# Who rounds and modulates the expert tokens: a second half moved to VectorE, a modulation spread over four steps

## What is computed

```python
def moe_swiglu(h, router_w, router_b, wg, wu, wd):
    logits = (h @ router_w).astype(jnp.float32) + router_b.astype(jnp.float32)
    top_val, top_idx = lax.top_k(logits, TOP_K)
    top_w = jax.nn.softmax(top_val, axis=-1)
    ...
    out = jnp.zeros_like(h)
    for e in range(N_EXPERTS):
        out = out + gates[..., e:e + 1] * swiglu(h, wg[e], wu[e], wd[e])
    return out
```

## Time and profile before

| | us |
|---|---|
| time, median of 3 runs (2276.32 to 2282.88) | 2277.53 |
| the profiled execution: its time | 2279.8 |
| the profiled execution: its span | 2278.0 |
| TensorE busy | 2151.4 (94% of the span) |
| VectorE busy | 1745.4 (77%) |
| ScalarE busy | 1329.2 (58%) |
| GpSimd busy | 116.7 (5%) |
| weight remainders on VectorE, L3227, 288 of 2.29 us | 654.8 |
| weight roundings on ScalarE, L2231, 288 of 1.91 us | 549.6 |

### The profile page before, as it was taken

One profiled execution on the slowest core, in us unless ns is written; L12 is line 12 of the kernel. 1 busy time (PEld: TensorE's weight loads), 2 busy tenths in 40 slices (PEclk: granted clock), 3 DMA queues, 4 the chain that ended last, 5 costly groups with the idle time before them and its releaser, 6 DMA issues.

```text
span 2278.0 us, 30568 instructions
## 1 busy us (share of the span) xinstructions
PE 2151.4 (94%) x11791; PEld 1825.7 (80%) x11791; DVE 1745.4 (77%) x1729; ACT 1329.2 (58%) x1394; POOL 116.7 (5%) x141
## 2 busy tenths in 40 slices
PE   6999989899999999999988799999999999999995
PEld 5977878789888696998876688888888888888884
DVE  6467677667774664677868688888998989898896
ACT  4654435555434423443563577777777777777774
POOL 2000000000010010001000100000000000000000
PEclk8999989999999999999999799999999999999998
DMA  8754663447876312768645599999999999999994
GB/s 324 261 188 166 214 220 138 153 156 254 300 264 244 128 63 75 268 234 303 226 172 202 207 369 357 397 348 403 350 396 356 392 362 381 374 375 375 370 379 165
DMA packets 249440, 621.27 MB, mean 273 GB/s; under 512 B 13658, under 2 KB 22213, under 8 KB 249285
## 3 DMA queue, kind: packets, MB, share of 16 engines
q1 hardware_dynamic: 229444, 530.28, 63.6%
q0 software_dynamic: 16864, 81.86, 10.2%
q10 hardware_dynamic: 3042, 7.88, 0.9%
HBM read 611.60 MB, written 12.58 MB: 274 GB/s over the span
## 4 chain that ended last, share of the span: by engine, by line
PE 79%; DVE 11%; ACT 4%; DMA 3%; issue 2%; POOL 0%; DVEq 0%; POOLq 0%; ACTq 0%
PE ps L1531 24%; PE ps L718 15%; PE ps L1536 12%; PE ps L760 8%; PE ps L741 5%; DVE ada L2273 2%; ACT w_high L2231 2%; DVE ring_low L2264 2%; PE ps L803 2%; DMA slab<-in_w_ada 1%; DVE arena L2264 1%; PE ps L1502 1%; DVE arena L3188 1%; DVE arena L2273 1%; DMA arena<-in_w_ada 1%
## 5 line engine op out<-in xcount | busy, mean ns | idle before, releaser
L3227 DVE TENSOR_TENSOR w_low<-ring,w_high 128x2048 fp32r<-128x2048 f32 x288 | 654.8, 2287 | 92.0 <-PE ps L1536 71.9
L2231 ACT CAST w_high<-ring 128x2048 fp32r<-128x2048 f32 x288 | 549.6, 1914 | 198.0 <-PE ps L1536 182.0
L1580 ACT CAST part_high<-ring 128x1024 fp32r<-128x1024 f32 x287 | 297.0, 1049 | 328.0 <-PE ps L760 137.7
L2264 DVE TENSOR_TENSOR ring_low<-ring,part_high 128x1024 fp32r<-128x1024 f32 x287 | 340.0, 1217 | 153.8 <-ACT part_high L1580 152.2
L1531 PE MATMUL ps<-w_high,tokens_hl 128*128 128x512 f32 x1792 | 449.3, 393 | 5.7 <-POOL tokens_hl L647 5.7
L1531 PEld LDWEIGHTS ps<-w_high,tokens_hl 128*128 128x128 f32 x1792 | 334.3, 188 | 74.6 <-issue 5.5
L760 PE MATMUL ps<-part_high,arena_split 128*128 128x512 f32 x752 | 237.7, 398 | 14.1 <-DVE arena_split L2264 6.1
L1536 PE MATMUL ps<-w_low,tokens_hl 128*128 128x512 f32 x896 | 240.2, 390 | 0.9 <-DVE w_low L3227 0.9
L1531 PE MATMUL ps<-w_high,hidden_hl 128*128 128x512 f32 x896 | 224.4, 392 | 0.0
L1536 PEld LDWEIGHTS ps<-w_low,tokens_hl 128*128 128x128 f32 x896 | 168.1, 188 | 37.1 <-DVE w_low L3227 1.4
L1531 PEld LDWEIGHTS ps<-w_high,hidden_hl 128*128 128x128 f32 x896 | 166.4, 188 | 34.4
(11 more groups left out here) (293 smaller groups left out, 2447.1 us busy)
## 6 DMA issues: line engine op xcount, KB each, us to landing
ring<-in_moe_w_gate SPq DMA_DIRECT2D x96, 1024.0 KB, 7.0
ring<-in_moe_w_up SPq DMA_DIRECT2D x96, 1024.0 KB, 6.8
ring<-in_moe_w_down SPq DMA_DIRECT2D x96, 1024.0 KB, 7.1
slab<-in_ada_w POOLq DMA_DIRECT2D x64, 768.0 KB, 5.6
ring<-in_w_in SPq DMA_DIRECT2D x22, 2048.0 KB, 8.9
ring<-in_w_ff SPq DMA_DIRECT2D x16, 2048.0 KB, 8.7
hT<-in_moe_w_up SPq DMA_DIRECT2D x16, 1024.0 KB, 6.9
hT<-in_moe_w_gate SPq DMA_DIRECT2D x16, 1024.0 KB, 7.3
```

The source lines that it names most:

```text
L1580: L(nc.scalar.copy(o, i), s)
L2231: nc.scalar.copy(high, whole).then_inc(sem("high_ready"), 1)
L2264: L(V.tensor_tensor(o, a, b, op), s)
L3227: V.tensor_tensor(low, whole, high.bitcast(F32), ALU.subtract).then_inc(sem("low_ready"), 1)
```

## The change

Four things are moved.

- **The first tokens' second half.** GpSimd rounds only tiles 0 to 3 of the first round's tokens. VectorE rounds tiles 4 to 7 and forms their remainder, behind its own modulation and ahead of its first weight remainder.
- **The modulation of the next round's tokens.** At steps 33 to 36 ScalarE modulates tiles 0 to 3, one per step, and VectorE tiles 4 to 7, one per step. ScalarE waits for the turned tokens (`gathered`) at step 33. At step 37 it also waits for its own last weight rounding (`high_ready`), by which its tiles are written.
- **The token remainders.** The first half stands at m = 38 as before, the second at m = 39.
- **Routing.** The first three count products signal `routed` 2 by themselves; the other two go to another PSUM bank and signal 3. The reduction of the counts on VectorE follows the selection instead of standing ahead of it, and waits for 3. An equality test and a product, one behind the other, become one operation for each of the two token tiles.

```diff
-            for h in range(2):
-                four = slice(4 * h, 4 * h + 4)
-                pool.wait_ge(sem("gathered_ready"), h + 1)
-                nc.gpsimd.tensor_copy(tokens_hl[:, 0, four], A(EG, KT, P)[:, four]).then_inc(sem("tokens_high"), 1)
-                pool.wait_ge(sem("tokens_high"), h + 1)
...
+            four = slice(0, 4)
+            pool.wait_ge(sem("gathered_ready"), 1)
+            nc.gpsimd.tensor_copy(tokens_hl[:, 0, four], A(EG, KT, P)[:, four]).then_inc(sem("tokens_high"), 1)
+            pool.wait_ge(sem("tokens_high"), 1)
...
-            pe.matmul(ps[:, 1, 8:16], con("until"), mask[:, 1, :], start=False, stop=True)
-            pe.matmul(ps[:, 1, 16:24], ones, mask[:, 0, :], start=True, stop=False)
-            pe.matmul(ps[:, 1, 16:24], ones, mask[:, 1, :], start=False, stop=True).then_inc(sem("routed"), 1)
+            pe.matmul(ps[:, 1, 8:16], con("until"), mask[:, 1, :], start=False, stop=True).then_inc(sem("routed"), 1)
+            pe.matmul(ps[:, 7, 0:8], ones, mask[:, 0, :], start=True, stop=False)
+            pe.matmul(ps[:, 7, 0:8], ones, mask[:, 1, :], start=False, stop=True).then_inc(sem("routed"), 1)
...
+            def modulated(n, k):
+
+                act.wait_ge(sem("gathered"), n)
+                nc.scalar.activation(A(EG, KT, P)[:, k, :], ps[:, 0, k * P:(k + 1) * P], ACT.Identity,
+                                     scale=shift[:, 1, k:k + 1], bias=shift[:, 1, KT + k:KT + k + 1])
...
+                    if 33 <= m < 37:
+                        modulated(i + 3, m - 33)
                     if m == 37:
+                        act.wait_ge(sem("high_ready"), i * E_STEPS + (m + 1))
                         gathered_high(i + 3)
...
-                tt(eq, lg, top[i].unsqueeze(2).broadcast_to([P, 2, 8]), ALU.is_equal)
-                L.settle()
-                tt(eq, eq, rank, ALU.mult)
+                for t in range(TT):
+                    stt(eq[:, t, :], lg[:, t, :], top[i][:, t:t + 1], con("eight_down"), ALU.is_equal, ALU.mult)
...
-            L(V.tensor_reduce(best[:, 0:1], ps[:, 1, 16:24], AX.X, ALU.max))
...
             build_selection(0).then_inc(sem("selected"), 1)
+            dve.wait_ge(sem("routed"), 3)
+            L(V.tensor_reduce(best[:, 0:1], ps[:, 7, 0:8], AX.X, ALU.max))
...
-                modulate(h + 1, range(4 * h, 4 * h + 4))
+                modulate(h + 1, range(4 * h, 4 * h + 4)).then_inc(sem("gathered_ready"), 1)
+            dve.wait_ge(sem("gathered_ready"), 2)
+            dve.wait_ge(sem("tokens_low"), 1)
+            V.tensor_copy(tokens_hl[:, 0, 4:8], gathered[:, 4:8]).then_inc(sem("tokens_high"), 1)
+            dve.wait_ge(sem("tokens_high"), 2)
+            V.tensor_tensor(tokens_hl[:, 1, 4:8], gathered[:, 4:8], tokens_hl[:, 0, 4:8].bitcast(F32), ALU.subtract
+                            ).then_inc(sem("tokens_low"), 1)
...
-                    if m == 36:
-                        modulate(i + 3, range(KT))
-                    if m == 38:
-                        gathered_low(i + 3)
+                    if 33 <= m < 37:
+                        ins = modulate(i + 3, (m - 29,))
+                        if m == 36:
+                            ins.then_inc(sem("gathered_ready"), 1)
+                    if m in (38, 39):
+                        gathered_low(i + 3, slice(4 * (m - 38), 4 * (m - 37)))
```

More of the change, by code:

```diff
@@ L640, in _ @@
                                                 ).then_inc(sem("kv_scaled"), 1)
-            for h in range(2):
-                four = slice(4 * h, 4 * h + 4)
-                pool.wait_ge(sem("gathered_ready"), h + 1)
-                nc.gpsimd.tensor_copy(tokens_hl[:, 0, four], A(EG, KT, P)[:, four]).then_inc(sem("tokens_high"), 1)
-                pool.wait_ge(sem("tokens_high"), h + 1)
-                nc.gpsimd.tensor_tensor(tokens_hl[:, 1, four], A(EG, KT, P)[:, four], tokens_hl[:, 0, four].bitcast(F32),
-                                        ALU.subtract).then_inc(sem("tokens_low"), 1)
+            four = slice(0, 4)
+            pool.wait_ge(sem("gathered_ready"), 1)
+            nc.gpsimd.tensor_copy(tokens_hl[:, 0, four], A(EG, KT, P)[:, four]).then_inc(sem("tokens_high"), 1)
+            pool.wait_ge(sem("tokens_high"), 1)
+            nc.gpsimd.tensor_tensor(tokens_hl[:, 1, four], A(EG, KT, P)[:, four], tokens_hl[:, 0, four].bitcast(F32),
+                                    ALU.subtract).then_inc(sem("tokens_low"), 1)
             pool.wait_ge(sem("vector2"), 6)
@@ L3189, in modulate, with gathered_low @@
                                           shift[:, 1, k:k + 1], shift[:, 1, KT + k:KT + k + 1], ALU.mult, ALU.add)
-                ins.then_inc(sem("gathered_ready"), 1)
-            def gathered_low(n):
+                return ins
+            def gathered_low(n, four):
                 dve.wait_ge(sem("tokens_high"), n)
-                for four in (slice(0, 4), slice(4, 8)):
-                    V.tensor_tensor(tokens_hl[:, 1, four], A(EG, KT, P)[:, four], tokens_hl[:, 0, four].bitcast(F32),
-                                    ALU.subtract).then_inc(sem("tokens_low"), 1)
+                V.tensor_tensor(tokens_hl[:, 1, four], A(EG, KT, P)[:, four], tokens_hl[:, 0, four].bitcast(F32),
+                                ALU.subtract).then_inc(sem("tokens_low"), 1)
             def copy_output(n_done, moved):
@@ L3232, in _ @@
                     if m == 12:
[L3233 removed]
+                        dve.wait_ge(sem("routed"), i + 4)
                         V.tensor_copy(rounds[:, 2 + 2 * TT:3 + 2 * TT], ps[:, 4, 0:1]).then_inc(sem("slot_tokens"), 1)
```

2 lines of the change are left out of this document (1 added, 1 removed).

## The result

| | us |
|---|---|
| changed kernel, median of 6 runs (2252.53 to 2264.65) | 2261.07 |
| kernel before beside it, median of 6 runs (2270.67 to 2282.88) | 2276.82 |
| ratio, with its 95% interval | 0.9941 [0.9921, 0.9962] |
| the profiled execution of the changed kernel: time, span | 2252.53, 2250.7 |

The kernel is faster, by 13.4 us as the ratio has it (8.7 to 18.0). 17.2 us had been forecast, as 2260.3 us.

The account below looks back on a forecast made before the run. TensorE was taken as the bound, with only small gaps to win: 6.0 us at the first round's start plus 11.2 in the rounds, 17.2 off 2277.5, gives 2260.3 us; range 2255 to 2268.

Parts of the forecast that it names:

- 11.2 forecast: Steps 37 to 39 of all eight rounds: the three stalls go, minus 11.2 us.
- the new wait of ScalarE: Step 33: ScalarE's first tile waits for the tokens turned by TensorE, 1.6 us once per round.
- the cover: Step 34: VectorE's remainder waits for TensorE until about 1385.7 anyway, so ScalarE's delay of 1.3 us stays hidden.
- No stall moved elsewhere: Rival, steps 38 to 40: token remainders cost 0.5 us per round, 4 us stay in, 2264.3 us; chance 0.12.
- DMA did not take over: Rival, rounds: DMA limits at 374 GB/s, a round stays at 120.4 us, only 6.0 won, 2271.5; chance 0.06.
- ScalarE did not become the bound: Rival, steps 33 to 37: table loads with the tiles make ScalarE the bound, 10.8 us slower, 2288.3; chance 0.03.
- The term of 6.0 us: First round's start: step 6 starts at about 1301.5 instead of 1307.47, minus 6.0 us.
- The start's own chain: First round: weight remainders start at 1283.72 against 1283.67, step 1 at 1287.15 instead of 1292.30.
- the full clock: First round's step 1, behind a gap of about 2 us: full clock taken, step 2 at 1289.87 instead of 1296.59.
- a sign of being wrong: Half clock in the first round's step 1; step 6 then at 1302.3, the start giving minus 5.2 us.
- The pairs of small routing operations: Routing: two dependent pairs become independent ones, 0.25 us instead of 0.38 each, so 0.26 go.
- the lower bound of 0.49: VectorE's new 128x512 rounding at the start: bounds 0.49 and 0.68 us, 0.49 taken.

Follow-up runs that it names:

- the run with extra tiles: Changed kernel, but ScalarE computes each of its four tiles three more times into places nobody reads; rounds of 120.27 us, 1.23 us lost per round.
- The experiment with the start alone: Changed kernel with the loop put back: changed routing and first tokens' rounding, rounds as before; 2269.82 us beside 2275.13, ratio 0.9968.
- the run with the rounding alone: Kernel before with only the rounding of the first tokens' second half moved to VectorE, routing and rounds as before; one run of 2270.97 us.
- the run with the order enforced: Kernel before plus one wait: VectorE waits, ahead of its first weight remainder, for GpSimd's second rounding; one run of 2271.17 us.

## Why the prediction was right, and where it was not

**The rounds: right in mechanism and size.** 11.35 us were won of 11.2 forecast, nearly all in steps 37 to 40. Of the working, step by step: the new wait of ScalarE 1.68 us (forecast 1.6), a tile on ScalarE 0.46, as in the earlier trace rows; VectorE's remainder of step 34 still waits for TensorE and not for ScalarE, so the cover held; the smallest spare time 1.1 us (step 40 of the first round) for a forecast 1.3. The remainder of step 37 started at 1378.42, for about 1378.7 forecast on this trace's scale (step 37 starts 15.63 us earlier here). No stall moved elsewhere. What the prediction did not see is that parts of this were not needed: once the modulation is spread, a round stays at 119.04 to 119.06 us without the second engine, and without the split of the token remainders (both left out at once was not tried).

**DMA did not take over.** The rounds moved 378 and 383 GB/s where the earlier trace rows has 374, and no wait of a weight rounding ended on a DMA. The 358 GB/s of the Trainium skill's page "DMA: Bandwidth & Descriptors" (Specifications), read as the prediction does as a limit of this core, would have held the round at 120.4 us or more; the trace disagrees by 20 to 25 GB/s.

**ScalarE did not become the bound,** by nearly 3 us of room per round, as the run with extra tiles showed. No table load came with the tiles.

**The start: right in this pair of traces, mis-sized for the kernel.** The term of 6.0 us took the start in the earlier trace rows as what the kernel before always does. It was one of two courses, and in the two further profiles of it the 7.01 us rounding was 0.60, and step 6 stood 5.5 us earlier. From those to the changed start with a short gather the gain is 32.5 - 31.2 = 1.3 us. With a long gather on both sides it is 38.03 - 33.10 = 4.9, and for the first pair of traces 6.9. That 6.9 lies near the forecast 6.0 is luck: the forecast had the long gather on both sides, the pair had it on one. A short gather before and a long one after would be 0.6 us lost. So the start gives anything from -0.6 to 7 us, by the course that each execution takes. Where all gathers are short, the routing alone brings some 0.7 of the 1.3 us (31.76 against 32.34 to 32.53), and the moved rounding the rest. The unchanged start met a long gather in one trace of four, which is too few for a share. An estimate from these traces: with a quarter to a third of long gathers before, and one in seven after (one of the seven traces of the changed start), the mean is 1.3 + 5.5 x 0.25 to 0.33 - 1.9 / 7, 2.4 to 2.9 us, and 11.3 + 2.7 = 14.0, inside both intervals. That fits the times; that it is this share and not another is not shown. The experiment with the start alone gave 7.3 us (3.9 to 10.5), of which 1.2 belong to its rounds, somewhat more than this.

**The start's own chain, and the clock.** The run with ScalarE's extra tiles has the changed start with the gather that the prediction reckoned with. Its first weight remainder began 14.49 us behind the logits (forecast 14.28), step 1 at 17.87 (17.71), step 6 at 33.10 (32.06). The chain held up to step 1. What failed there is the full clock that the prediction took for step 1 behind a gap of about 2 us, by the earlier trace rows. TensorE in steps 0 and 1 of that run:

```profile
1283.91 1.20 PE L1535 MATMUL ps<-w_low,tokens_hl 128*128 128x512 f32 x4 [2.09 <-DVE w_low L3246]
1284.95 3.30 PE L1530 MATMUL ps<-w_high,tokens_hl 128*128 128x512 f32 x8
```

Behind 2.09 us of idle time the eight matmuls of step 1 took 3.30 us, most of it at a granted 0.50, as in the run with the rounding alone. The prediction had named this as a sign of being wrong, with step 6 then at 32.9. The profile of the changed kernel does not show it, since its gap was 0.95 us.

Inside the start of the changed kernel's own profile, four sizes were off. The pairs of small routing operations became 0.02 us shorter each, not 0.13: 0.36 us for a pair, since a pair of these three-operand ones does not overlap as the two in the earlier trace rows did. So the gather begins 0.97 us earlier, not 1.20. The rounding on VectorE took 0.43, below the lower bound of 0.49. VectorE's wait for GpSimd's first remainder bound by 0.39 us; the prediction named no cost for it. And the gather was 1.46 us shorter, which no one had changed. The first weight remainder began 13.35 us behind the logits instead of the forecast 14.28, step 1 came 4.1 us behind step 0 instead of 5.2, and step 5's stall was 0.31 instead of 0.6.

**The time itself.** 2261.07 and 2260.99 us lie 0.8 us from the forecast, by luck: the gain was 4 to 5 us smaller than forecast, and the median that it was taken from, 2277.53, stood 0.7 to 3.7 us above the 2276.82, 2275.13 and 2273.79 of the later comparisons.

## What to carry to other kernels

Where TensorE waits at a few steps of a loop, look for a block of side work put behind one step on an engine that has spare time in each of its neighbours, and spread it; whether a second engine helps is a second question, and here it did not. Before a stall at a start that runs once is counted as a gain, look in a second and third profile whether it is always there: an order of two engines that is not enforced can turn on a few tenths of a microsecond. And count times of two traces from a point behind the last unchanged work.

## What the runs showed of the hardware that was not expected

**The gather of 32 equal matmuls takes 5.2 to 5.8 us (eleven traces) or 6.8 (three),** by when the granted clock goes from 0.50 to 1.00 within it. Stages of 1 us, of the changed kernel and of the run with ScalarE's extra tiles, each from 3 us behind the start of its gather (1265.92 and 1272.29):

```profile
1268.90:1269.90 1.00, 1.00 (x10) 1.00 (x10) 0.40 (x2) 0.00 (x0) 0.00 (x0) 0.96 0.00 0
1269.90:1270.90 1.00, 1.00 (x11) 1.00 (x10) 0.97 (x4) 0.81 (x1) 0.00 (x0) 1.00 0.33 119
```

```profile
1275.20:1276.20 1.00, 1.00 (x7) 1.00 (x6) 0.09 (x1) 0.00 (x0) 0.00 (x0) 0.50 0.00 0
1276.20:1277.20 1.00, 1.00 (x7) 1.00 (x7) 1.00 (x4) 0.73 (x1) 0.00 (x0) 0.50 0.30 61
```

These are the levels of 1.2 and 2.4 GHz: six or seven matmuls per us, or ten or eleven. Both have the same instructions ahead and the same gap of 0.22 us. What decides the moment is open; the gap does not, since gathers behind 1.14 us of idle time were also of both lengths (6.75 and 6.79; 5.20, 5.31, 5.39, 5.45).

**GpSimd beside VectorE.** Its rounding of 128x512 took 0.60 us when it began 0.26 us ahead of VectorE's remainder, and 7.01 when it began 0.15 behind the earlier trace rows, to 0.48 us past the end of all three. The Trainium skill's page "SBUF — State Buffer" (SBUF: two separate sides) says that the two share a pair of ports, which VectorE needs for an operation with two inputs in SBUF, as its remainders are, when GpSimd reads SBUF too, and that whoever starts first has it for the whole instruction while the other waits. The 0.60 agrees, and so does VectorE's first remainder behind GpSimd's in the run with the order enforced, 3.19 us instead of 2.28. The 7.01 goes beyond it: three remainders passed, not one. GpSimd's own two-operand remainder, begun behind VectorE's first, took 3.22 us instead of 1.27, and VectorE's three 7.99 instead of 6.68: 2.49, 3.38 and 2.28 us, so it is the second that is a whole 1.1 us longer, as if GpSimd had gone in between the first and the second. Why the rounding could not and the remainder could was not tried.
